# Output stage of a hybrid encoder block: shift row written ahead, accumulating stores, scale row and deviation on other engines

## What is computed

```python
def layer_norm(x, g, b):
    xf = x.astype(jnp.float32)
    mu = jnp.mean(xf, axis=-1, keepdims=True)
    var = jnp.mean(jnp.square(xf - mu), axis=-1, keepdims=True)
    y = (xf - mu) * lax.rsqrt(var + LN_EPS) * g.astype(jnp.float32) + b.astype(jnp.float32)
    return y.astype(x.dtype)
...
        h = layer_norm(DEEPNORM_ALPHA * h + gt2[:, None, :] * ff, ln2_g[l], ln2_b[l])
    return h
```

## Time and profile before

| | us |
|---|---|
| median of 3 runs | 1973.94 (1973.82 to 1976.06) |
| the profiled execution, its own time | 1973.8 |
| span of that execution in the trace | 1972.0 |
| output stage, from the first load's issue to the end of the span | 1914.73 to 1972.0 |
| busy over the span | PE 1821.8, DVE 1433.9, ACT 1069.5, POOL 358.7 |

### The profile page before, as it was taken

The page is one execution under the profiler, slowest core; times in us unless marked ns, Lnnn a source line. Parts: engine busy times, 40 slices in busy tenths (PEclk is TensorE's granted clock), DMA queues, the critical chain, the costliest instruction groups (busy, mean ns, idle before and its releaser), DMA issues. The chain is left out here.

```text
span 1972.0 us, 35312 instructions
## 1 busy us (share of the span) xinstructions
PE 1821.8 (92%) x14136; PEld 1036.1 (53%) x14136; DVE 1433.9 (73%) x1790; ACT 1069.5 (54%) x1310; POOL 358.7 (18%) x230
## 2 busy tenths in 40 slices
PE   4999989999969999989999999489999999999965
PEld 1656644444459999954444455344444444444432
DVE  5555656858766666626765778689999988888938
ACT  3466643465433333333333311288888888888934
POOL 0000000111001211200000000124444444444400
PEclk9999999999989999999999999589999999999988
DMA  8500045752463232033314121399999999999935
GB/s 324 104 22 23 1 164 190 252 197 104 172 150 93 51 98 51 3 108 99 107 54 139 33 94 67 133 393 391 409 406 413 409 398 401 391 390 387 370 144 202
DMA packets 161716, 391.32 MB, mean 198 GB/s; under 512 B 25371, under 2 KB 102804, under 8 KB 132910
## 3 DMA queue, kind: packets, MB, share of 16 engines
q1 hardware_dynamic: 146574, 357.87, 50.2%
q0 software_dynamic: 15008, 31.56, 4.2%
HBM read 361.68 MB, written 48.68 MB: 208 GB/s over the span
## 5 line engine op out<-in xcount | busy, mean ns | idle before, releaser
L2281 PE MATMUL ps<-w_gate_up_split,gathered_t 128*128 128x512 f16 x1728 | 388.4, 382 | 9.0 <-ACT gathered_t L2355 5.4
L2447 DVE SCALAR_TENSOR_TENSOR w_gate_up_split<-w_staged,w_gate_up_split 128x2048 f16<-128x2048 f32 x144 | 328.2, 2289 | 58.4 <-ACT w_gate_up_split L2346 57.0
L2346 ACT ACTIVATE w_gate_up_split<-w_staged 128x2048 f16<-128x2048 f32 x144 | 274.6, 1908 | 46.6 <-PE ps L2281 16.0
L2281 PEld LDWEIGHTS ps<-w_gate_up_split,gathered_t 128*128 128x128 f16 x1728 | 167.9, 98 | 209.1 <-ACT gathered_t L2355 10.6
L219 PE MATMUL ps<-u_transposed,w_gates_split 128*128 128x512 f16 x1152 | 254.8, 383 | 5.7 <-PEq L144 3.0
L825 PE MATMUL ps<-u_transposed,w_dense_split 128*128 128x512 f16 x1152 | 250.5, 379 | 1.7 <-DVE w_dense_split L190 0.9
L2308 PE MATMUL ps<-w_down_split,hidden_t 128*128 128x512 f16 x864 | 193.9, 381 | 7.2 <-ACT hidden_t L2392 4.5
L219 PEld LDWEIGHTS ps<-u_transposed,w_gates_split 128*128 128x128 f16 x1152 | 113.3, 99 | 146.8 <-issue 15.0
L825 PEld LDWEIGHTS ps<-u_transposed,w_dense_split 128*128 128x128 f16 x1152 | 111.9, 98 | 142.3 <-issue 7.1
L2447 DVE SCALAR_TENSOR_TENSOR w_down_split<-w_staged,w_down_split 128x2048 f16<-128x2048 f32 x72 | 164.2, 2287 | 17.1 <-ACT w_down_split L2346 16.9
L2346 ACT ACTIVATE w_down_split<-w_staged 128x2048 f16<-128x2048 f32 x72 | 137.3, 1908 | 44.4 <-DMA w_staged<-in_w_down 22.9
(11 more groups left out here) (359 smaller groups left out, 2923.2 us busy)
## 6 DMA issues: line engine op xcount, KB each, us to landing
w_staged<-in_w_gate SPq DMA_DIRECT2D x72, 1024.0 KB, 11.5
w_staged<-in_w_up SPq DMA_DIRECT2D x72, 1024.0 KB, 10.9
w_staged<-in_w_down SPq DMA_DIRECT2D x72, 1024.0 KB, 10.9
w_dense_ring<-in_w_in SPq DMA_DIRECT2D x17, 1024.0 KB, 7.6
w_ada_ring<-in_w_ada SPq DMA_DIRECT2D x8, 2048.0 KB
w_gates_ring<-in_w_in SPq DMA_DIRECT2D x24, 512.0 KB, 6.5
qkv_scratch<-delta_output POOLq DMA_DIRECT2D x20, 512.0 KB, 3.4
attention_output<-qkv_scratch SPq DMA_DIRECT2D x8, 1024.0 KB, 6.1
```

The costliest lines, as they stand in the source:

```text
L2281: last = pe.matmul(ps[:, GU[s] + j, :], xt[:, s, xp, k, :], w16[:, j, wp, k, :], start=(k == 0 and t == 0), stop=(k == KC - 1 and t == 2))
L2346: nc.scalar.activation(split(kind, 0, int(q)), staged(m, kind, int(q)), ACT.Identity, scale=W_SCALE).then_inc(hi_ok[kind + q], 1)
L2447: nc.vector.scalar_tensor_tensor(split(kind, 1, int(q)), staged(m, kind, int(q)), W_SCALE, split(kind, 0, int(q)), ALU.mult, ALU.subtract) ...
```

## The change

The result is now built in two parts. During the delta rule, SP issues one DMA that writes the shift row `ln2_b` into all 1024 rows of the output (4 MB, memory to memory); SP waits for its landing at the end of that block. In the output stage, what is left of the norm is added to those rows: POOL stores each chunk with a DMA that adds to what the memory holds (`accum_op=ALU.add`). SP's stores are gone. The work on a chunk is also cut differently: DVE multiplies (value − mean) by the scale row in one instruction as soon as it has the mean, and ACT then divides by the deviation, in place. The instruction that added the shift row, the product of mean and reciprocal, and the load of the shift row in `route` are removed, and `m.tail_rows` holds two rows in place of three. The wait for the store of three chunks before (`out_done`) moves from ACT to DVE, in front of the new product.

```diff
@@ delta_rule, SP
+        out_filled = m.sem("out_filled_with_shift")
...
                 if c == 2:
                     load_gates(m, a, sp, 0)
+                if c == 4:
+                    sp.dma_start(out[0], a["ln2_b"].to_broadcast([T, D])).then_inc(out_filled, 16)
+            sp.wait_ge(out_filled, 16)
@@ route, SP
-            sp.dma_start(m.tail_rows[:, 1, :], a["ln2_b"].to_broadcast([P, D])).then_inc(tail_in, 16)
-            sp.dma_start(m.tail_rows[:, 2, :], m.ada_dram[5:6, :].to_broadcast([P, D])).then_inc(tail_in, 16)
-            sp.wait_ge(tail_in, 48)
+            sp.dma_start(m.tail_rows[:, 1, :], m.ada_dram[5:6, :].to_broadcast([P, D])).then_inc(tail_in, 16)
+            sp.wait_ge(tail_in, 32)
@@ experts, SP
-            for c in range(TC):
-                sp.wait_ge(res_ok, c + 1)
-                sp.dma_start(out_view[:, c, :], res[:, c % 3, :]).then_inc(out_done[c % 3], 16)
-            for s in range(3):
-                sp.wait_ge(out_done[s], 16 * len(range(s, TC, 3)))
@@ experts, POOL
             pool.sem_inc(all_stored, 1)
+            for c in range(TC):
+                pool.wait_ge(scaled_ok, c + 1)
+                pool.dma_start(out_view[:, c, :], res[:, c % 3, :], accum_op=ALU.add).then_inc(out_done[c % 3], 16)
+            for s in range(3):
+                pool.wait_ge(out_done[s], 16 * len(range(s, TC, 3)))
@@ experts, ACT
-            def unit(c):
-                act.wait_ge(shift_ok, c + 1)
-                if c >= 3:
-                    act.wait_ge(out_done[c % 3], 16 * (c // 3))
-                nc.scalar.activation(res[:, c % 3, :], m.z1[:, c, :], ACT.Identity, scale=rstd[:, c:c + 1], bias=shift[:, c:c + 1]
-                                     ).then_inc(unit_ok, 1)
+            def scale(c):
+                act.wait_ge(product_ok, c + 1)
+                act.wait_ge(rstd_ok, c + 1)
+                nc.scalar.activation(res[:, c % 3, :], res[:, c % 3, :], ACT.Identity, scale=rstd[:, c:c + 1]).then_inc(scaled_ok, 1)
             for c in range(TC):
                 moments(c)
                 if c >= 1:
-                    unit(c - 1)
-            unit(TC - 1)
+                    scale(c - 1)
+            scale(TC - 1)
@@ experts, DVE
                 nc.vector.tensor_scalar(mean[:, c:c + 1], tot[:, 0, c:c + 1], -1.0 / D, None, ALU.mult).then_inc(mean_ok, 1)
+                dve.wait_ge(mean_ok, c + 1)
+                if c >= 3:
+                    dve.wait_ge(out_done[c % 3], 16 * (c // 3))
+                nc.vector.scalar_tensor_tensor(res[:, c % 3, :], m.z1[:, c, :], mean[:, c:c + 1], rows[:, 0, :], ALU.add, ALU.mult
+                                               ).then_inc(product_ok, 1)
             def scalars(c):
                 dve.wait_ge(std_ok, c + 1)
-                step(nc.vector.reciprocal(rstd[:, c:c + 1], std[:, c:c + 1]))
-                step.settle()
-                nc.vector.tensor_tensor(shift[:, c:c + 1], mean[:, c:c + 1], rstd[:, c:c + 1], ALU.mult).then_inc(shift_ok, 1)
-
-            def scale(c):
-                dve.wait_ge(unit_ok, c + 1)
-                step(nc.vector.tensor_tensor(res[:, c % 3, :], res[:, c % 3, :], rows[:, 0, :], ALU.mult))
-                step.settle()
-                nc.vector.tensor_tensor(res[:, c % 3, :], res[:, c % 3, :], rows[:, 1, :], ALU.add).then_inc(res_ok, 1)
-
-            for c in range(TC + 1):
-                if c < TC:
-                    sums(c)
+                nc.vector.reciprocal(rstd[:, c:c + 1], std[:, c:c + 1]).then_inc(rstd_ok, 1)
+
+            for c in range(TC):
+                sums(c)
                 if c >= 1:
                     scalars(c - 1)
-                if c >= 2:
-                    scale(c - 2)
-            scale(TC - 1)
+            scalars(TC - 1)
```

More of the change, by code:

```diff
@@ L1092, in _, with delta_rule @@
                 pool.wait_ge(ada_out[b], 16 * 3)
-def delta_rule(nc, m, a):
+def delta_rule(nc, m, a, out):
     with ExitStack() as ctx:
@@ L2130, in experts @@
         rstd = m.sb("ln2_rstd", [P, TC], ctx=ctx)
-        shift = m.sb("ln2_minus_mean_rstd", [P, TC], ctx=ctx)
         eps = m.sb("ln2_eps", [P, 1], ctx=ctx)
-        mean_ok, std_ok, shift_ok, unit_ok, scaled_ok, added, sum_used, dve_p, act_p = (m.sem("combine_" + n) for n in (
-            "mean_ready", "std_ready", "shift_ready", "unit_ready", "scaled", "choices_added", "rows_used", "dve_steps", "act_steps"))
+        mean_ok, std_ok, rstd_ok, product_ok, scaled_ok, added, sum_used, dve_p, act_p = (m.sem("combine_" + n) for n in (
+            "mean_ready", "std_ready", "rstd_ready", "product_ready", "scaled", "choices_added", "rows_used", "dve_steps", "act_steps"))
         all_stored = m.sem("moe_all_stored")
         y_in = [m.sem(f"combine_y_in{s}") for s in range(RING)]
-        res_ok = m.sem("combine_result_ready")
         out_done = [m.sem(f"combine_stored{s}") for s in range(3)]
@@ L2504, in sums @@
                 nc.vector.tensor_tensor(yc.rearrange("p (h n) -> p h n", h=2), ps[:, 2 * (c % 4):2 * (c % 4) + 2, :],
-                                        rows[:, 2, :].rearrange("p (h n) -> p h n", h=2), ALU.mult).then_inc(sum_used, 1)
+                                        rows[:, 1, :].rearrange("p (h n) -> p h n", h=2), ALU.mult).then_inc(sum_used, 1)
                 dve.wait_ge(sum_used, c + 1)
@@ L2589, in build @@
                 m.gate_hi, m.gate_lo, m.gate_mm = (nc.alloc_semaphore(name="gates_" + n) for n in ("high_ready", "low_ready", "summed"))
-                delta_rule(nc, m, a)
+                delta_rule(nc, m, a, out)
                 attended.close()
@@ L2594, in build @@
                 merge(nc, m, a)
-            m.tail_rows = tail.enter_context(nc.sbuf_tensor("ln2_gate2_rows", [P, 3, D], F32, side="right"))
+            m.tail_rows = tail.enter_context(nc.sbuf_tensor("ln2_gate2_rows", [P, 2, D], F32, side="right"))
             m.stage = late.enter_context(nc.sbuf_tensor("w_staged", [P, 6, 2048], F32, side="right"))
```

## The result

| | before | after |
|---|---|---|
| median of 4 runs, us | 1974.6 (1973.8 to 1976.1) | 1987.54 (1984.45 to 1993.68) |
| after / before | | 1.0067, 95% interval 1.0048 to 1.0087 |
| profiled execution, us | 1973.8, span 1972.0 | 1993.68, span 1991.8 |
| output stage, first load issued to the end of the span, us | 1914.73 to 1972.0: 57.3 | 1928.08 to 1991.8: 63.7 |

The change makes the kernel 0.67% slower, 12.9 us by the medians. I had forecast 1967.9 us, a gain of 6.0, and a range that ended at 1983.0; the time lies above it. The profiled execution of the changed kernel is 6.1 us above its own median, so its trace shows more loss than the median does: 3.2 us were already there before the fill began (the decay rows of piece 4 issued at 656.52, against 653.31 before), which no part of the change explains.

A forecast was written before the change was run, and what follows sets the result against it. DVE was taken to bound the output stage, all on the ending path. Last chunk finished at 1959.5, plus waits 0.6 and store tail 5.9, gave 1966.0 instead of 1972.0: 1973.9 − 6.0 = 1967.9 us, range 1965.3 to 1983.

The forecast's parts named there:

- DVE's share: Output stage: two wide instructions and a small one go, one of 1.22 us comes; 3.93 us a chunk instead of 5.25.
- The tail of chunk 7: End of the output stage: 6.65 us from chunk 7's start to its scaling's end at 1959.5, 9.4 us earlier than before.
- The stores: After ACT's last scaling: 0.3 us to POOL's start, 5.1 to landing, 0.5 behind it; 5.9 us, 2.8 longer than before.
- the same 0.5: Time from the last store's landing to the end of the span, taken as 0.5 us, unchanged from before.
- L: Landing time of an accumulating 512 KB store from POOL, taken as 5.1 us, between 3.4 and 9.7.
- the ring eats the gain: Rival: first stores share DMA engines with expert loads, landing in 5.8 to 7.6 us; change not measurable; chance 0.10.
- each microsecond of L costs four: Beyond 5.1 us, DVE's waits at chunks 3, 5 and 7 and the last landing each grow by the excess.
- What is hidden: Delta rule: the 4 MB fill, 10 or 21.1 us, fits 26.7 us before SP's queue's next issue; costed at nothing.
- My rival on the fill: Delta rule: the fill is not hidden, costing from about 50 us of duration; at 60 us, time 1978; chance 0.03.
- POOL and DVE in each other's way: Rival, output stage: accumulating stores suffer 0.7 us beside DVE's wide instructions; time 1970.7, gain 3.2, within 0.2%; chance 0.07.
- Slower: accumulating is slow in itself: Rival: adding to memory runs far below copy rate, DVE waits ahead of the product; up to 1986.3 us; chance 0.22.

The follow-up runs named there:

- the mixed version: Changed kernel with chunks 0 to 3 accumulated by POOL, 4 to 7 finished on DVE and stored by SP, fill in four parts, ring of four: 1967.15 us, ratio 0.9956.
- the ring of four: Changed kernel with the fill in eight parts, and four result buffers in place of three: 1978.04 us, ratio 1.0015.

## Why the prediction was wrong

The direction was wrong, and the mechanism that decides is in none of my rivals. By my own steps, set against the profiled execution from DVE's first instruction of the stage (1925.45 before, 1939.24 after) to the end of the span: I forecast 46.55 − 6.0 = 40.5 us, and it was 52.6. The gap of 12.0 us has three terms.

**"DVE's share" was right.** A product of 1.28 for the forecast 1.22, a pitch of 3.92 to 3.97 for 3.93. From the first instruction of chunk 0 to that of chunk 7 are 31.54 us; less the two waits in between (3.17 and 0.68) 27.7, where I had 27.4. PE was no bound.

**"The tail of chunk 7" was right as far as it went.** From chunk 7's start (1970.78) to the end of its scaling (1975.48 + 2.19 = 1977.67) are 6.9 us with its wait of 0.59, so 6.3; forecast 6.65.

**"The stores": the last term, "the same 0.5", failed.** I took what lay behind the last landing as a constant of the program. It is a property of the engine that is last. Measured: 1984.95 to 1991.8, 6.85 us. That is 6.35 us of the gap. POOL's drain shows this; waiting with POOL in the old kernel costs 6.6 by the median with no other change, and the mixed version, where POOL is done early, has its 3.1 us from the last DVE instruction to the end again. My section on the change costed every instruction that POOL was given and not that it is now in the block to its end.

**"The stores": L was mis-sized twice.** I took 5.1 for all stores, from the plain 3.4 and a share of DMA that was low *before*. A quiet one takes 5.2 to 5.6 (the slowest: issue at 1959.84, landing at 1965.42), close to it. The first, issued while expert results still came in at a share of 1.01, took 8.1 (1948.79 to 1956.84), which is the rival "the ring eats the gain" at one place: 3.2 us of wait. The last took 7.0; the one before had been issued only 1.04 us earlier, since chunk 7's scaling follows chunk 6's at once. That this is the reason isn't shown: in all these kernels the last two are this close. Waits 4.4 for 0.6 (+3.8), last landing 7.0 for 5.1 (+1.9). I had used a share of 0.25, a row of a kernel without accumulating stores; with them it was 0.77. The rule that each microsecond of L costs four didn't apply, since L was not one number.

6.35 + 3.8 + 1.9 make the 12.0. (The terms that I call right come to +0.3 for DVE's share and −0.35 for the tail, and cancel.)

**"What is hidden": the fill costed at nothing failed.** The duration came out above both of my figures (10 and 21.1 us; measured 24.8, and 26.5 in the kernel with the fill alone), and it still fitted the gap of 26.7 us on SP's queue. But I asked only which *loads* of the program it could delay. It delayed one that stands on no queue of the program, PE's instructions, and then the idle time cost PE its clock for a while. Measured alone, +8.6 us; in eight parts, 0 in the pitches and −6.8 in the time. My rival on the fill had the right place and the wrong mechanism: it was to begin at 50 us of duration, and had 0.03. Together, 12.0 in the output stage and 6.8 for the fill make 18.8; from the forecast −6.0 to the measured +12.9 are 18.9. That these agree to 0.1 us is partly luck: the 12.0 are read from one execution, 6.1 us above the median, and the 6.8 are a difference of medians. In that execution's span, 19.8 us longer than before, 3.2 us lie ahead of the fill, 8.5 in the delta rule, 1.6 between it and the output stage, 0.4 ahead of DVE's first sum and 6.0 behind it; the cause of the 3.2 and of the 1.6 I don't know.

**"POOL and DVE in each other's way"** didn't show: POOL issued its stores in 0.85 to 0.98 us, beside DVE's products, and these kept their 1.28.

**"Slower: accumulating is slow in itself"** held in part: an addition to memory costs some 2.3 us over a plain store when quiet (5.2 to 5.6 against 2.9 to 3.3) and 5.9 us of the stage. With the drain taken off, that alone would have eaten the gain: the stage of the changed kernel less its drain is 63.7 − 6.4 = 57.3 us, that of the kernel before; with the ring of four it is 61.3 − 6.4 = 54.9, a gain of 2.4 (estimates: no kernel here has all eight accumulated and the drain hidden).

**Open:** why POOL's drain takes 5.8 us with nothing under way; why the second gap of PE under the fill comes in some executions only; why the last of eight accumulating stores takes 7.0 us in some kernels and 8.8 in others.

## What to carry to other kernels

Before the last work of a block is given to another engine, read that engine's own row at the block's end in the trace: a cost that is hidden while the engine is done early comes onto the path whole; here its 6.4 us were more than the forecast gain of 6.0. A large transfer that fits a gap between loads still competes with the streams of instructions; cut it into pieces, or put it where the engines need few instructions a microsecond. If a slow kind of store buys time on a busy engine, use it for the first chunks and leave the last ones to the quick kind: with the fill cut up, that turned a loss of 12.9 us into a gain of 8.9 by the medians.

## What the runs showed of the hardware that I had not expected

- At a block's end POOL's drain lasted 5.78 us where POOL had issued no stores in the stage (9.1 where the row covers its last addition of 3.26 too), 6.44 behind landed stores, and 8.4 to 12.1 with its own transfers still under way; in those three kernels it ended 3.1 to 3.2 us behind the last landing of POOL's own. SP's lasted 0.007 us in the runs that end on it.
- A DMA from memory to memory that held a DMA share of 0.91 to 1.03 left PE without instructions for 2.1 and 1.5 us in a stage of 64x64 products, and the granted clock at 0.72 over the 18 us around the second gap; in four kernels the gaps stood before the same two matmuls and ended 1.1 to 1.4 us behind the landing of a 16 KB packet of instructions; in a stage of 128x512 products nothing happened.
- Accumulating stores of 512 KB landed in 5.2 to 5.6 us alone, 8.1 beside loads, and 7.0 or 8.8 for the last, issued 1.04 us behind another; plain ones of the same queue in 2.9 to 3.3, and 6.6 beside loads. POOL needed 0.86 us to issue one, 0.98 for the first, and 0.54 for a plain one. The accumulating ones held a DMA share of 0.77 for 128 GB/s.
- A DVE product of two SBUF operands took 3.07 us instead of 1.28 beside POOL's addition, which itself took 3.27, and an instruction of the same kind that had begun just before POOL's kept its 1.22.
